# GLA chunk outputs on column tiles of 32, placed directly behind the next chunk's scores

## What is computed

```
def gla_chunked(q, k, v, log_a, s0):      # per head; the kernel uses chunks of 128
    b = jnp.cumsum(gc, axis=1)
    scores = jnp.einsum('bihd,bjhd,bijhd->bhij', qc, kc, exp(b_i - b_j), causal)
    o = (jnp.einsum('bhij,bjhe->bihe', scores, vc)
         + jnp.einsum('bihd,bhde->bihe', qc * jnp.exp(b), s))
    s = (s * jnp.exp(b_last)[..., None]
         + jnp.einsum('bjhd,bjhe->bhde', kc * jnp.exp(b_last[:, None] - b), vc))
```

## Time and profile before

| | us |
|---|---|
| median of 3 runs | 2394.71 (2394.4 to 2396.81) |
| the profiled execution's own time | 2400.48 |
| its span in the profile | 2398.5 |
| PE busy | 2376.1 (99%) |
| DVE busy | 1317.3 (55%) |
| ACT busy | 795.9 (33%) |
| mean granted clock | 0.996 |

### The profile page before, as it was taken

One profiled execution on the slowest core, in us unless ns is written; L12 is line 12 of the kernel. 1 busy time (PEld: TensorE's weight loads), 2 busy tenths in 40 slices (PEclk: granted clock), 3 DMA queues, 4 the chain that ended last, 5 costly groups with the idle time before them and its releaser, 6 DMA issues. The chain is left out here.

```text
span 2398.5 us, 44934 instructions
## 1 busy us (share of the span) xinstructions
PE 2376.1 (99%) x17600; PEld 2334.0 (97%) x17600; DVE 1317.3 (55%) x2069; ACT 795.9 (33%) x1254; POOL 1221.6 (51%) x1445
## 2 busy tenths in 40 slices
PE   9999999999999999999999999999999999999998
PEld 9999989999999999999989999999999999999998
DVE  6764353345545545556587776643345545545566
ACT  4711431222222222232444665532223223223234
POOL 2454226566666666677311111356466666666681
PEclk9999999999999999999999999999999999999999
DMA  4123031111111111113212112131111111111112
GB/s 153 36 64 90 27 121 45 42 47 45 51 47 45 54 45 45 54 36 109 73 46 74 48 46 74 53 114 46 43 54 39 50 53 42 47 53 44 45 53 84
DMA packets 41025, 140.14 MB, mean 58 GB/s; under 512 B 6321, under 2 KB 10033, under 8 KB 39697
## 3 DMA queue, kind: packets, MB, share of 16 engines
q1 hardware_dynamic: 32768, 106.78, 13.5%
q10 hardware_dynamic: 8080, 30.78, 3.6%
HBM read 120.42 MB, written 14.88 MB: 56 GB/s over the span
## 5 line engine op out<-in xcount | busy, mean ns | idle before, releaser
L742 PE MATMUL PS<-RB,WH 128*128 128x384 f32 (+1 forms) x4368 | 1083.9, 329 | 0.0
L742 PEld LDWEIGHTS PS<-RB,WH 128*128 128x128 f32 x4368 | 770.4, 188 | 5.9 <-issue 2.1
L742 PE MATMUL PS<-RA,WH 128*128 128x272 f32 (+2 forms) x3520 | 769.6, 309 | 3.1 <-DVE RA L2124 1.2
L742 PE MATMUL PS<-RB,WL 128*128 128x384 f32 (+1 forms) x2232 | 730.0, 327 | 0.0
L648 POOL TENSOR_TENSOR WH<-WR,FEW 128x256 fp32r<-128x256 f32 x420 | 323.4, 801 | 609.4 <-PE PS L742 579.9
L742 PEld LDWEIGHTS PS<-RA,WH 128*128 128x128 f32 x3520 | 587.4, 188 | 7.7 <-DVE RA L2596 1.4
L742 PE MATMUL PS<-RA,WL 128*128 128x272 f32 (+2 forms) x1760 | 540.6, 307 | 0.0
L742 PEld LDWEIGHTS PS<-RB,WL 128*128 128x128 f32 x2232 | 419.8, 188 | 0.0
L652 POOL TENSOR_TENSOR WL<-WR,WH 128x256 fp32r<-128x256 f32 x420 | 375.2, 923 | 0.0
L742 PEld LDWEIGHTS PS<-RA,WL 128*128 128x128 f32 x1760 | 330.9, 188 | 0.0
L1984 DVE TENSOR_TENSOR X<-PS,X 128x544 f32<-128x544 f32 x280 | 202.5, 724 | 204.6 <-PE PS L742 204.5
(11 more groups left out here) (239 smaller groups left out, 2306.0 us busy)
## 6 DMA issues: line engine op xcount, KB each, us to landing
WR<-ws SPq DMA_DIRECT2D x189, 512.0 KB, 3.5
EB<-xT ACTq DMA_DIRECT2D x8, 544.0 KB, 6.3
x_spill<-X ACTq DMA_DIRECT2D x8, 544.0 KB, 2.9
EB<-x_spill ACTq DMA_DIRECT2D x8, 544.0 KB, 6.4
GA<-st_gla ACTq DMA_DIRECT2D x4, 1024.0 KB, 4.8
glas_o<-GA ACTq DMA_DIRECT2D x4, 1024.0 KB, 4.0
yT<-X SPq DMA_DIRECT2D x16, 208.0 KB, 1.9
X<-xT ACTq DMA_DIRECT2D x4, 544.0 KB, 6.4
```

The lines of the kernel that those rows point to most:

```text
L742: return nc.tensor.matmul(out, lhsT, rhs, start=start, stop=stop, skip_group_check=True)
```

## The change

The outputs of every full chunk are computed as four matmuls with 32 stationary columns each, into 32 partitions each, in place of one with 128. `go_done` is raised once for each of the four tiles, as it already was for the sample chunk. In the list, both halves that a place hands out early now stand ahead of the next place's scores (one, where this place is the sample chunk), `L` stands ahead of the transposes, and the half between scores and outputs is gone, so the outputs follow the scores directly on TensorE.

```diff
@@ odd_schedule
             if not last:
-                s += (take(1) if p == 8 else []) + [("A",) + PLACES[k + 1]] + take(1)
-                s.append(("A2",) + PLACES[k + 1])
+                s += take(1) if p == 8 else []
                 if lines is not None:
                     s.append(("L", h + 1, lines))
+                s += [("A",) + PLACES[k + 1]] + take(1 if c == LAST else 2)
+                s.append(("A2",) + PLACES[k + 1])
                 if k + 1 == len(PLACES) - 1:
                     s += [("MIX", 0), ("MIX", 1)]
...
                 if last:
                     s += [("MIX", 3), ("MH", 4), ("MH", 5), ("MEH", 6)] + take(2)
-                elif not norm or len(half) > 1:
-                    s += take(1)
                 s += ([] if norm else prep[0]) + [("B", h, c)]
@@ build
         def written(places):

-            return sum(P // BLOCK if c == LAST else 1 for _, c in PLACES[:places])
+            return P // BLOCK * places
@@ TensorE, item B
                     if c:
                         for v in range(2):
-                            mm(PS[:, 6, 128 * v:128 * (v + 1)], gST[:, 128 * v:128 * (v + 1)], gQD[e % 2][:, loc:loc + n],
-                               v == 0, False)
+                            for r in range(0, P, BLOCK):
+                                mm(PS[r:r + BLOCK, 6, 128 * v:128 * (v + 1)], gST[:, 128 * v + r:128 * v + r + BLOCK],
+                                   gQD[e % 2][:, loc:loc + n], v == 0, False)
                     for v in range(2):
-                        last = mm(PS[:, 6, 128 * v:128 * (v + 1)], kvt[:, 128 * (v + 1):128 * (v + 2)], gSC[k % 2],
-                                  c == 0 and v == 0, v == 1)
-                    last.then_inc(go_done, 1)
+                        for r in range(0, P, BLOCK):
+                            last = mm(PS[r:r + BLOCK, 6, 128 * v:128 * (v + 1)], kvt[:, 128 * (v + 1) + r:128 * (v + 1) + r + BLOCK],
+                                      gSC[k % 2], c == 0 and v == 0, v == 1)
+                            if v:
+
+                                last.then_inc(go_done, 1)
```

## The result

The changed kernel takes 2403.4 us (median of 6 runs, 2401.11 to 2406.61) against 2395.14 for the kernel before (6 runs on the same chip, 2394.16 to 2398.29): ratio 1.0034, 95% interval 1.0023 to 1.0044, so 8.3 us slower. The forecast was 2403.1.

A forecast was written before the change was run, and what follows sets the result against it. TensorE, busy for 355.3 of the GLA stage's 360 us, was taken to set the time. Terms 4.5 + 4.9 - 1.2 + 1.9 - 4.2 + 1.6 + 1.6 - 0.7 gave +8.4 on the median 2394.7: 2403.1 us, range 2395 to 2410.

The forecast's parts named there:

- column tiles: Outputs on tiles of 32: a place from scores to update takes 1.86 instead of 1.72, +4.5 us for 32 places.
- L behind the head sum: Heads 1 and 2: six gate logits directly behind the head sum wait for ScalarE's logarithm, 0.82 each, +4.9 us.
- update no longer behind L's read: Output and update at four places: the update stops waiting for the read of L's bank, -1.2 us.
- head sum directly behind the update, places 9 and 18: The head sum waits for VectorE's state copy out of bank 7, 0.95 at each of two places, +1.9 us.
- waits inside scores gone: Three places stop waiting inside scores for VectorE's Q products, since scores come one half later, -4.2 us.
- head 0's first head sum: Head 0, place 4: TensorE arrives early and waits for the state update behind VectorE's chain, +1.6 us.
- go_copied at the sample chunks: Last chunks of heads 0, 1, 2 wait for ScalarE's copy of the chunk before, 0.5 to 0.6 each, +1.6 us.
- rival 1: Exit from the output tiles is hidden: a place costs -0.07 instead of +0.14, total 2396.4 us; chance 0.13.
- rival 2: VectorE's chain gives nothing back: all 4.2 us stay won, both +1.6 terms don't come, 2399.9 us; chance 0.12.
- rival 3: Output tiles overlap only in part, 3.1 of 4: +0.26 for each of 30 full-size places, 2410.9 us; chance 0.08.
- rival 5: Output tiles fill while scores run, saving 0.45 in 32 places, -14.4 us, total 2388.7 us; chance 0.06.
- rival 4: New stops near a sample chunk bring another stretch at half clock into each run, +3.4, 2406.5 us; chance 0.08.

The follow-up runs named there:

- test 1: The changed kernel with its outputs full-width again (8 records of 128x128 in a chunk, one signal), new order kept: 2403.59 us, ratio to the kernel before 1.0031.
- test 3: The kernel before, in its own order, with only the outputs put on column tiles of 32: 2399.63 us, ratio to the kernel before 1.0010.
- test 2: The changed kernel with L one half projection later, behind the transposes and the first half, tiles kept: 2397.23 us, ratio to the kernel before 1.0001.
- test 5: The changed kernel with full-width outputs and L one half projection later, together: 2397.82 us, ratio to the kernel before 1.0008.
- test 7: The changed kernel with full-width outputs, L one half later, and a half between update and head sum at places 3, 9, 18: 2395.49 us, ratio to before 0.9994.
- test 9: test 7's kernel with the outputs of places 19 and 20 only on column tiles of 32: 2392.16 us, ratio to the kernel before 0.9986.
- test 4: The changed kernel with outputs on two column tiles of 64 instead of four of 32, order unchanged: 2407.54 us, ratio to the kernel before 1.0044.
- test 8: The kernel before with the second half ahead of the scores at places 2, 14, 23 and L ahead of the scores everywhere: 2394.43 us, ratio 0.9992.
- test 10: test 7's kernel with outputs on column tiles of 32 everywhere except places 19 to 22: 2399.33 us, ratio to the kernel before 1.0012.
- test 11: test 8's kernel with the outputs of places 18 and 23 on column tiles of 32: 2391.72 us, ratio to the kernel before 0.9982.
- test 12: test 7's kernel with sixteen waits on a long-raised semaphore ahead of the transposes of each of places 18 to 23: 2395.87 us, ratio to before 1.0001.

## Why the prediction was right, step by step

The forecast was +8.4, the runs say +8.3 with an interval of 5.5 to 10.5, so that the times agree within 0.3 us (2403.1 and 2403.4) is luck. The main mechanisms were right (tiles that pay at their exit, L behind the logarithm, waits inside the scores gone), but three sizes were not (tiles, L, go_copied), and their errors cancel. "Measured" is from the starts of TensorE's records in the two profiles, place by place, without the stop and the stretches at half clock.

| step | forecast | measured |
|---|---|---|
| column tiles | +4.5 | +3.9: 0.14 to 0.17 in most places, about 0 in 5 |
| L behind the head sum | +4.9 | +5.6 |
| L itself in its new place | 0 | +0.6 |
| update no longer behind L's read | -1.2 | -1.2 |
| head sum directly behind the update, places 9 and 18 | +1.9 | +2.0 |
| waits inside scores gone | -4.2 | -4.2 |
| head 0's first head sum | +1.6 | +1.4 |
| go_copied at the sample chunks | +1.6 | +0.6 |
| absorbed, small waits | -0.7 | -0.3 |
| sum (of unrounded terms) | +8.4 | +8.3 |

- *Column tiles.* The mechanism and the size of a place are right (1.85 for 1.86): tests 1 and 3 show 0.14 in the new order and 0.29 in the old. All 32 were priced alike, but the four places behind a sample chunk's scores, and the first chunk of head 0, change by -0.04 to +0.03. *Order alone* is worth nothing, as forecast: test 1's 0.74 + 0.97 = 1.71 equals the 1.71 of before.
- *L.* Right in kind, and test 2 gave it all back. It was undersized: L follows the logarithm's end by 0.14 where 0.06 were forecast, and the logarithm itself starts 0.55 behind the head sum, not 0.50. Besides, L was taken to cost the same anywhere: between scores and half it lengthened T's way by 0.14 to 0.18, ahead of the transposes by 0.24 to 0.27.
- *Head sums.* Right. The update's step is 1.11 and 1.26 longer at places 9 and 18, and 0.16 to 0.19 of each was paid before, at the half that stood behind the update. In head 0 the step is 1.86 longer, and 0.49 of it was paid before in the same way, 0.29 of that as a wait for the same state update.
- *go_copied.* This step failed in heads 1 and 2. There the sample chunk has six halves, and one of them stays between scores and outputs (`if len(half) > 3`). In head 1 the copy, at 1341.53 between exponentials, was done by 1341.89, the outputs came at 1342.19. In head 0, without that half, +0.59 came as forecast.
- *"The change does not touch" the stretch at half clock.* This failed as well, and is what the prediction did not see at all. The earlier trace rows shows 6.9 us at 0.51 in head 2's sample chunk, and ahead of them T stood for 0.55 us with nothing to wait for. It was taken for chance. The stop belongs to the count of T's instructions, which the tiles moved by some 980 there; whether the half clock does is not shown. Taking the tiles out again (tests 1, 5, 7) gains 2 to 3 us in the places and next to nothing in the time; the stop, which comes back with full-width outputs, and the clock would make up for it, but that they do so in the unprofiled runs is only argued. So the tiles' price is shown by the places and not by the time. The two profiles alone show +5.8 for the stage: +8.3, less 4.1 for the stop and the half clock of before, and 1.5 more for the half clock of after. How much of its 2395 the kernel before pays for its stop in a usual run isn't known: its mean loss to the clock (6.6 to 7.9) is nearer to test 9's (7.0) than to test 7's (9.4).
- *Rivals.* 1 fell: T leaves the tiles for 0.20, 0.09 over the stream, and 0.10 more at the update. 2 held in part: the chain gave back 2.0 of the 3.2 (1.4 and 0.6). 3 fell: 3.6 us of stream pass in 0.92, 3.9 of 4 (in test 4, with two tiles of 64, 1.9 of 2). The Trainium skill's figure in "TensorE: Matmul & The Clock Gate", Measured speedup vs the span model, is 2.38x for three column tiles, there with 512 moving columns; the trace does not agree for 128. 5 fell: no output started before the last score. 4 had the wrong sign here: this change moved a stop away from a sample chunk, and its runs lost no more to the clock (7.2) than those of the kernel before (6.6 to 7.9).

## What to carry to other kernels

A change of tile shape costs at its exit (here 0.20 us) and where tiles begin behind full-width work (0.06), so count the changes; splitting a stationary matrix that is full already buys nothing. An instruction that reads what another engine derives from the matmul just ahead of it stops TensorE for that engine's whole step: one half projection (2.1 us) between them hid 0.93. The copy of an update out of its bank is such a case too (1.1 to 1.3 us at places 9 and 18). And a change of the number of instructions can move a stop that belongs to the count: where a profile shows TensorE idle for nothing inside a run of short matmuls, shift the count before you judge an edit, and judge it by its places as well as by its time.

## What the runs showed of the hardware that I had not expected

- TensorE stopped for 0.31 to 1.76 us, with nothing to wait for, 8 times in 14 profiles at a sample chunk, always at a record 195 above a multiple of 256 and only where that record lay 240 to 272 behind the start of 256 short ones; in the other 48 sample chunks (the number 36 to 228 behind the start) never. Why is not shown; that the supply of instructions falls behind in such a run is only argued. Not every stop that the profile puts down to "issue" fits: one of 0.55 to 0.60 in layer 0, in six of the profiles, stands at record 3682, which leaves 98.
- Near six of the eight stops TensorE ran at half clock, 1.2 GHz instead of 2.4, for 3.4 or 6.8 us. It fell at the stop's end or up to 1.3 us behind it in three (before, tests 1 and 7), within the stop in two (test 4 at 1256.0, test 10 at 1432.1), and 1.0 us ahead of it in test 8. At the stop of test 5 and the second of test 4 it kept 1.00. And half clock also came at a sample chunk without a stop, in the change at 1255, in tests 5 and 10 in head 0, and in test 11 (PE's window below, directly behind a sample chunk that ran through), and in test 4 at 1392.5, far from any. So the stops and the half clock are not one thing, and what brings the second stays open.

```profile
1427.40:1430.80 3.40, 3.40 (x13) 3.33 (x12) 3.26 (x11) 1.59 (x4) 0.00 (x0) 0.55 0.00 0
```

- A wait for what has long happened costs time on TensorE's own list: in test 12 96 of them make 48 records 0.10 to 0.11 us apart. Where other work covered them they cost nothing that the trace shows, at place 19 T stood for 0.55 us.
